# Sixteen gate tiles of a branch moved from the layer norm of token block 1 into four longer turns of its convolution

## The reference, cut to what matters

```python
h = _rmsnorm(x, norm1_g[l])
proj = h @ w_in[l]
q, k, v, og, gkf, gkb, glu, ga, gb = jnp.split(proj, offsets, axis=-1)
...
o = _rmsnorm(o, gla_onorm_g[l])
o = (o * jax.nn.silu(og...)).reshape(B, S, GLA_VAL_WIDTH)
y_a = o @ gla_w_o[l]
a_in, a_gate = jnp.split(glu, 2, axis=-1)
u = a_in * jax.nn.sigmoid(a_gate)
u = lax.conv_general_dilated(u, conv_w[l][:, None, :], ...) + conv_b[l]   # 31 taps
u = jax.nn.silu(_layernorm(u, conv_ln_g[l], conv_ln_b[l]))
y_b = u @ conv_w_pw2[l]
merged = jax.nn.sigmoid(ga) * y_a + jax.nn.sigmoid(gb) * y_b
x = x + merged @ w_out[l]
h2 = _rmsnorm(x, norm2_g[l]).reshape(B * S, D)
x = x + _peer(h2, peer_w_q[l], peer_keys[l], peer_u[l], peer_v[l]).reshape(B, S, D)
```

## Time and profile before

| what | us |
|---|---|
| median of three executions | 4335.33 |
| their range | 4331.25 to 4346.49 |
| the profiled execution | 4332.04 |
| its span, first to last instruction | 4330.1 |
| TensorE busy | 3728.1 (86%) |
| VectorE busy | 2641.5 (61%) |
| ScalarE busy | 890.5 (21%) |
| GpSimd busy | 773.6 (18%) |
| DMA engines, mean rate | 354 GB/s, 1531.06 MB |

### The profile page before, as it was taken

One profiled execution on the slowest core, in us unless ns is written; L12 is line 12 of the kernel. 1 busy time (PEld: TensorE's weight loads), 2 busy tenths in 40 slices (PEclk: granted clock), 3 DMA queues, 4 the chain that ended last, 5 costly groups with the idle time before them and its releaser, 6 DMA issues. The chain is left out here.

```text
span 4330.1 us, 39650 instructions
## 1 busy us (share of the span) xinstructions
PE 3728.1 (86%) x13710; PEld 2248.7 (52%) x13710; DVE 2641.5 (61%) x3888; ACT 890.5 (21%) x2065; POOL 773.6 (18%) x525
## 2 busy tenths in 40 slices
PE   9999999999999999766799698758888887777777
PEld 3444489446666667663687586334444442322222
DVE  3132258103899999765767877886665664544444
ACT  2233210101122211242111111122222222212112
POOL 0000000000133332332221311222121121212111
PEclk9999999999999999888899899879999999999999
DMA  3111258888899999999999999999999999999998
GB/s 143 59 59 58 74 179 301 299 314 307 334 367 379 389 416 405 403 411 414 426 425 426 417 417 426 426 397 427 413 427 428 428 417 428 423 428 429 428 429 367
DMA packets 142779, 1531.06 MB, mean 354 GB/s; under 512 B 15312, under 2 KB 21584, under 8 KB 22096
## 3 DMA queue, kind: packets, MB, share of 16 engines
q0 software_dynamic: 73728, 1073.77, 59.1%
q1 hardware_dynamic: 67248, 445.32, 26.7%
q10 hardware_dynamic: 1696, 10.62, 0.6%
HBM read 1525.46 MB, written 4.19 MB: 353 GB/s over the span
## 5 line engine op out<-in xcount | busy, mean ns | idle before, releaser
L1730 PE MATMUL bank<-arena_h,wring 128*128 128x128 f32 (+5 forms) x6656 | 1389.3, 372 | 121.7 <-DVE arena_h L1448 46.3
L1730 PEld LDWEIGHTS bank<-arena_h,wring 128*128 128x128 f32 x6656 | 1029.1, 196 | 477.0 <-issue 188.1
L622 POOL DMA_INDIRECT arena_c<-in_peer_uv,arena_c x256 | 510.3, 1994 | 2495.0 <-DVE arena_o L1380 1338.1
L1371 DVE SCALAR_TENSOR_TENSOR arena_c<-arena_c 128x2048 f32<-128x2048 f32 x256 | 586.3, 2290 | 180.5 <-DMA arena_c<-in_peer_uv,arena_c 180.2
L2121 PE MATMUL bank<-arena_c,arena_h 128*128 128x512 f32 x1024 | 476.1, 608 | 158.7 <-ACT arena_h L996 158.7
L1380 DVE SCALAR_TENSOR_TENSOR arena_o<-arena_c,arena_o 128x2048 f32<-128x2048 f32 x234 | 550.1, 2351 | 68.2 <-ACT arena_c L804 61.4
L2088 PE MATMUL bank<-arena_c,cols 128*128 128x512 f32 x1024 | 473.1, 606 | 92.5 <-ACT cols L954 92.4
L1644 DVE SCALAR_TENSOR_TENSOR arena_c<-arena_c 128x2048 f32<-128x2048 f32 x128 | 293.4, 2292 | 332.8 <-DMA arena_c<-in_peer_uv,arena_c 332.6
L802 ACT ACTIVATE arena_c<-arena_c 128x1 f32<-128x1 f32 x384 | 77.8, 203 | 1918.8 <-DVE arena_c L1371 1426.9
L635 POOL DMA_INDIRECT arena_c<-in_peer_uv,arena_c x256 | 261.1, 1020 | 1034.4 <-PE bank L2088 525.5
L1590 DVE SCALAR_TENSOR_TENSOR arena_c<-arena_c 128x2048 f32<-128x2048 f32 x128 | 293.4, 2292 | 239.4 <-DMA arena_c<-in_peer_uv,arena_c 238.5
(11 more groups left out here) (227 smaller groups left out, 2627.5 us busy)
## 6 DMA issues: line engine op xcount, KB each, us to landing
wring<-in_w_in SPq DMA_DIRECT2D x176, 1024.0 KB, 10.1
wring<-in_w_out SPq DMA_DIRECT2D x48, 1024.0 KB, 11.1
wring<-in_peer_w_q SPq DMA_DIRECT2D x48, 1024.0 KB, 11.7
wring<-in_gla_w_o SPq DMA_DIRECT2D x32, 1024.0 KB, 14.7
wring<-in_conv_w_pw SPq DMA_DIRECT2D x32, 1024.0 KB, 15.7
wring<-in_w_v SPq DMA_DIRECT2D x16, 1024.0 KB, 4.9
wring<-in_w_ga SPq DMA_DIRECT2D x16, 1024.0 KB, 4.9
wring<-in_w_o_quarters SPq DMA_DIRECT2D x16, 1024.0 KB, 4.9
```

The lines of the kernel that those rows point to most:

```text
L622: pool.indirect_dma_start(out=slot_of(n), out_offset=None, in_=uv_tab, in_offset=at)\
L1371: V.scalar_tensor_tensor(row, row, 1.0, block_of(h2, n // P), ALU.mult, ALU.mult, accum_out=act_u[:, n % TOP:n % TOP + 1]).then_inc(dotted, 1)
L1730: last = M(ps[bank][:, at:at + hi - lo], w_tile(slot)[:, k, :], act_in[:, k, lo:hi], start=k == 0, stop=k == KT - 1)
```

## The change

The sixteen gate tiles of the second branch of block 1 are computed in the first four loops of TensorE, four a loop, between the og tiles and the tiles of the next turn. They go to banks 4 and 5, so they wait until og tiles of the same loop have been scaled, and the loop ends with a wait for the two sigmoids. The weight loads follow that order. ScalarE computes the two sigmoids at the steps 8 and 9 of a turn instead of behind the turns and between the squares. The first four turns hold 11, 12, 12 and 11 steps instead of 10, 11, 11 and 10, and all later turns start four steps later. The steps of the layer norm follow the turns more closely: XC_AT by 3 steps later than before and not 4, PW_AT by 2, NORM1_AT by 2, QUERY1_AT by 1, M2_AT not at all. The total of rows, tiles and bytes is as before.

```diff
-SB_MA1 = SB_OG1 + 32
+SB_MA1 = SB_OG1 + 48
 SB_MA1_LAST = SB_MA1 + 36
-SB_GB1 = SB_MA1_LAST + 8
-SB_PW1 = SB_GB1 + 16
+SB_PW1 = SB_MA1_LAST + 8
...
-TURN_AT = (4, 14, 25, 36, 46, 55, 64, 73, 81)
+TURN_AT = (4, 15, 27, 39, 50, 59, 68, 77, 85)
 OG_AT = (4, 7)
 IT_AT = (2, 5)
-X1_AT = 80
-GB_AT = 79
-XC_AT, SQUARE_AT = 84, 85
-RSTD_AT, ROOT_AT, RECIP_AT = 89, 89, 90
-SCALE1_AT, SILU1_AT = 91, 91
-PW_AT = 95
-SCALE2_AT, SILU2_AT = 96, 97
-RES1_AT = (103, 105, 107, 109)
-NORM1_AT = 110
-QUERY1_AT = 115
-FIND_AT = 5
+GB_AT = (8, 9)
+X1_AT = 84
+XC_AT, SQUARE_AT = 87, 88
+RSTD_AT, ROOT_AT, RECIP_AT = 92, 92, 93
+SCALE1_AT, SILU1_AT = 94, 94
+PW_AT = 97
+SCALE2_AT, SILU2_AT = 98, 99
+RES1_AT = (105, 107, 109, 111)
+NORM1_AT = 112
+QUERY1_AT = 116
+FIND_AT = 6
...
             with sp.Fori(0, 4) as j:
-                loads(SB_OG1, j, 8, w_in, j * 4 + WOG, 4)
-                loads(SB_OG1 + 4, j, 8, w_in, j * 2 + (WGATE + 2), 2)
-                loads(SB_OG1 + 6, j, 8, w_in, j * 2 + (WGLU + 2), 2)
+                loads(SB_OG1, j, 12, w_in, j * 4 + WOG, 4)
+                loads(SB_OG1 + 4, j, 12, w_in, j * 4 + WGB, 4)
+                loads(SB_OG1 + 8, j, 12, w_in, j * 2 + (WGATE + 2), 2)
+                loads(SB_OG1 + 10, j, 12, w_in, j * 2 + (WGLU + 2), 2)
...
-            row_loads(SB_GB1, w_in, WGB)
...
             def mb1_gates(n):
                 p = pair["mb1"]
                 act.wait_ge(p["gate"], n + 1)
-                A(sgb1[:, 2 * n:2 * n + 2, :], two(4 + n % 4, P), ACT.Sigmoid).then_inc(p["sig"], 1)
+                A(sgb1[:, 2 * n:2 * n + 2, :], two(4 + n % 2, P), ACT.Sigmoid).then_inc(p["sig"], 1)
...
+                    if j < 4 and r in GB_AT:
+                        mb1_gates(2 * j + GB_AT.index(r))
...
-                if 0 <= s - GB_AT < 4:
-                    mb1_gates(s - GB_AT)
...
-                if 0 <= s - (SQUARE_AT + 1) < 4:
-                    mb1_gates(4 + s - (SQUARE_AT + 1))
...
                 for n in range(4):
                     pe.wait_ge(og1["used"], j * 4 + (n + 1))
-                    tile_ready(SB_OG1 + n, j, 8)
+                    tile_ready(SB_OG1 + n, j, 12)
                     project(SB_OG1 + n, hT, 4 + n, P, T).then_inc(og1["mm"], 1)
-                glu1(SB_OG1 + 4, j, 8, 1, j)
+                for a in range(2):
+                    pe.wait_ge(og1["used"], j * 4 + (4 + a + 1))
+                    two_tiles(SB_OG1 + 4 + 2 * a, j, 12, hT, 4 + a, P, 2 * P).then_inc(pair["mb1"]["gate"], 1)
+                glu1(SB_OG1 + 8, j, 12, 1, j)
+                pe.wait_ge(pair["mb1"]["sig"], j * 2 + 2)
...
-            def mb1_gate(n):
-                if n >= 4:
-                    pe.wait_ge(pair["mb1"]["sig"], n - 3)
-                two_tiles(SB_GB1 + 2 * n, None, 0, hT, 4 + n % 4, P, 2 * P).then_inc(pair["mb1"]["gate"], 1)
-
-            pe.wait_ge(pair["ma1"]["use"], 2 + 8)
-            for n in range(4):
-                mb1_gate(n)
             pe.wait_ge(pair["glu1"]["use"], 2 + KT)
             pe.wait_ge(cv1_done, KT)
...
-                mb1_gate(4 + n)
+            pe.wait_ge(pair["ma1"]["use"], 2 + 8)
```

## The result

The changed kernel takes 4353.8 us (median), the kernel before, beside it, 4334.8; the ratio is 1.0038, with a 95% interval of 1.0025 to 1.005. That is slower by a little more than the 0.3% named in the prediction; 4348 us was forecast, 4330 to 4368 was the range. The profiled execution took 4352.3 us (span 4350.6), 20.5 us of span more than before.

The account below looks back on a forecast made before the run. TensorE, level with VectorE, was taken to bound the first four turns, transfers the rest from 1480 us. 52 + 5 - 33 - 15 = +9, with +4 for weight waits +13; 4335.3 + 13 = 4348 us, range 4330 to 4368.

Parts of the forecast that it names:

- The bound: First four turns: TensorE and VectorE level, TensorE without a gap; from 1480 us on, transfers are the floor.
- Part 1: First four turns: four gate tiles lengthen each TensorE loop from 81.0 to 95.3 us; turn 4 taken at 1532.8, +52 us.
- The waits for weights: First four turns: TensorE waits for tile loads in the longer loops, 1 us a loop taken, +4 us.
- Rival (a): Longer turns: transfers pace them, four small tiles in a row costing 4 to 8 us a loop; 4360 to 4376, chance 0.15.
- the prediction's own signs: First four turns: gaps in TensorE's piece of matmuls that end on a weight load would show transfers pacing the turns.
- the piece that was to run to about 1540: First four turns: TensorE's matmuls without a gap, expected from 1112 to about 1540 us.
- The new waits on the og tiles and the sigmoids: First four turns: TensorE's waits for scaled og tiles and, at the loop's end, for sigmoids cost nothing.
- Part 2: Turn 4: TensorE loses its 5 us lead and starts with the take; the loop lasts 79.3 us, +5 us.
- Part 3: Layer norm without gate tiles: 67.5 us from the taps' end to the pointwise projection instead of 100.8, -33 us.
- Part 4: Pointwise projection to first merge of the last blocks: three rows fewer, 6.3 MB at 421 GB/s, -15 us.
- Rival (c): Steps 97 to 116: three rows fewer don't pay, transfers pause; 4355 to 4363, chance 0.12 together with another rival.
- The 358 GB/s of memory: First four turns: a skill's memory limit for one core would cost 30 to 40 us more; given no chance.

Follow-up runs that it names:

- e4_gates_alone: The changed kernel with the first four turns at their old 10, 11, 11 and 10 rows, gate tiles still in them; 4367.4 us, ratio 1.0076.
- e1_gate_columns: The changed kernel with only 2 of the 16 matmuls computed for each of the sixteen gate tiles, loads unchanged; 4355.8 us, ratio 1.0043.

## Why the prediction was right, and where it was not

- **The bound and Part 1 (+52).** Right in mechanism and in size: with the bytes of the bunch cut, and no wait left, the tiles of turn 4 are ready at 1533, and 1532.8 was the sum; with the bunch broken up they are ready at 1532.6, after an earlier start. A loop of TensorE without gaps does hold the turns: with the bytes cut VectorE waits 34.9 us in the takes, and some 35 were expected. In the change it is 44.5, since the waits for weights come on top.
- **The waits for weights (+4).** Mis-sized: 5.4 us of waits and, behind two of them, 1.7 us each of slower matmuls, together 9; the tiles were ready 10 us after the sum without waits. The prediction counted the room by mean rate (396 GB/s against 413), named the 10.7 us that the load behind the bunch has, and took 1 us a loop, for the waits alone; the slow matmuls behind a wait were in no term. What decides is the lead of the tile behind the bunch. Rival (a) gave this mechanism, with 4 to 8 us a loop, which was too much. By the prediction's own signs it is part of the truth: gaps that end on a weight load were to speak for it, and the piece that was to run to about 1540 has three. The take of turn 4 (1542.8) is late for the 1533 to 1541 named, and the four turns ran at 376 GB/s, not at 380 to 390.
- **The new waits on the og tiles and the sigmoids (0).** Right: no gap of TensorE in the four turns ends on ScalarE or VectorE.
- **Part 2 (+5).** Did not happen. Turn 4 lasts from 1542.8 to 1616.4, 73.6 us, where 79.3 was taken over from before. TensorE waits 5.0 us for weights in it (0.97, 2.31 and 1.70) and not 8.2 (3.54, 2.92 and 1.70), the tile that took 5.47 us behind the longest of these waits takes the usual 3.7 to 3.8, and TensorE comes out level with VectorE, which needs as long for its nine rows. This error of 5 us and the one of 5 us on the waits for weights cancel, so that the lag behind the taps is the forecast's. That is luck: no step of the prediction ties the two together.
- **Part 3 (-33).** Right: 66.9 us from the step behind the taps to the projection, 67.5 forecast. The sum of the taps, after 33.7 us without work, took 12.07 us, 1.6 more than in the earlier trace rows, and no step waited for it. The granted clock is 0.56 from 1836 to 1840 and 1.00 from 1840 to 1848. By the rule of the Trainium skill that the prediction named (TensorE: Matmul & The Clock Gate, section on the HAM clock gate), only the beginning of the sum is slow; the trace agrees.
- **Part 4 (-15).** This is the step that failed: 7 us and not 15. It was worked out at 421 GB/s "if the transfers remain the bound, as 421 GB/s says". That figure was a mean over 329 us. The rows went ahead of TensorE's tiles (at step 131 the lag is only 7.0 us), VectorE reached the merge of step 132 early and waited there 24 us instead of 11, and the transfers fell to 385 and then 418 GB/s. From the projection to step 163, 6.4 MB less are moved than before, the three rows, but in only 9.1 us less (535.7 for 544.8): 6 us of the 15 are lost to the lower rate. Moving three merges took 6.6 us' worth of that away. Rival (c) named such a loss, but at steps 97 to 116; it lay at 132. The sign set for it, a lag at the first merge that is not 15 us below the one at the projection, is what came.
- **The total.** +20.5 us in the profile and +19 in the medians, where +13 was forecast. The whole of the difference is Part 4; up to the projection the sum is right by two errors that cancel.
- **The 358 GB/s of memory.** The prediction gave no chance to what the Trainium skill (DMA: Bandwidth & Descriptors, Where 436 GB/s comes from) puts as the memory side's limit for one core. The four turns ran at 376 GB/s after, at 388 with half of the gate tiles, and the last 1,388 us at 425: the trace disagrees with that section, and no run here was held by such a limit.

## What to carry over

A move into a stage where two engines are full costs its whole length, unless it is split so that each place takes what fits: against the longer turns alone (1499.9), half of the tiles moved the take of turn 4 by 3.5 us (1503.5) and all of them by 43 (1542.9). When short tiles stand in a row in a ring of weight slots, look at the lead of the long tile behind them: it is the time that the engine spends on the short ones (10.7 us here, and next to nothing when their matmuls were cut), and the long tile's load has to land in it. One long tile between pairs took the waits from 5.4 to 1.1 us. And price a wait by the rate of the bounding resource in it: removing 11 us of idle VectorE at 427 GB/s gained nothing that could be measured, while 24 us with 385 GB/s around them cost 3 us and as much again behind them, by the bytes that were not moved.

## What was not expected of the hardware

Some short waits of TensorE were paid twice. Behind waits of 1.87 and 2.18 us the same matmuls took 1.7 us longer (48.78 for 47.09 us, 192 of them; 97.21 for 95.52, 384 of them). The granted clock, TensorE's clock as a share of the full one, is 0.83 from 1402 to 1412 and from 1501 to 1511 and 1.00 in the 10 us behind each: part of these matmuls ran at 1.2 GHz, the lower of the two levels. Not every such wait does it. Behind one of 1.33 us in the same run, and behind 1.68 and 2.02 us in e4_gates_alone, the matmuls kept their 95.3 to 95.5 us a loop. What tells the waits apart stays open. With the gate tiles cut to almost nothing, loops with 5.5 to 13 us of waits took some 85 us for matmuls that take 82.5 without. In the run with the columns alone cut (e1_gate_columns) the granted clock over the four turns is 0.93. That is part of the reason why doing less on TensorE gave nothing back there.
